# A two-model transformer kernel on one core: first shift by TensorE products, first loads in another order, split latent norm, last expert's outputs one after the other

## The chip, the cores and the metric

The kernel runs on one core of a Trainium2 chip. The metric is the device time of one execution in microseconds (us). Three executions were timed; the median counts. A separate execution was taken by the hardware profiler.

## The reference

Two small transformers of two layers each, one after the other, on 256 tokens of width 1024, all in float32. What matters here:

```python
# first model, layer 0 (ada: shift, scale, gate from the condition c)
mod  = silu(c) @ ada_w[0] + ada_b[0]            # 6 x 1024 values: sh1, sc1, g1, ...
h    = rms_norm(x, attn_norm) * (1 + sc1) + sh1
x    = x + g1 * sparse_mixer(h, ...)            # h @ sp_w_in, attention, @ sp_w_out
...
# second model, layer 0: a pooling branch beside latent attention
proj = u @ in_w                                 # pool | query latents | key-value latents | k_rope
q    = rms_norm(q_lat, q_norm) @ q_up           # 8 heads of 96, rotated
k, v = rms_norm(kv_lat, kv_norm) @ kv_up
y    = concat([pool(...), attend(q, k, v)]) @ out_w
h    = layer_norm(alpha * h + g1 * y)
...
# second model, layer 1: 8 experts, top 2
out  = sum_e combine[:, e] * (silu(t @ wg[e]) * (t @ wu[e])) @ wd[e]
h    = layer_norm(alpha * h + g2 * out)
```

## The kernel before

The activations lie feature-major: `X` is 128 partitions x 8 tiles x 256 tokens. Each engine has its own hand-written program in one block, and semaphores alone order them. SyncE (SP) issues nearly all weight loads, in the order in which they stand in its program; its DMA queue fills a ring `wring` of six chunks of 2 MB. GpSimd (POOL) issues the loads of the ada rows through a ring of two half chunks. Most large products are done in three parts with rounded operands: ScalarE (ACT) makes a rounded copy of half a weight chunk (`round_part`), VectorE (DVE) subtracts it to get the remainder (`part_rest`), and TensorE (PE) multiplies rounded by rounded, rounded weights by the remainder of the activations, and the other way round (`by_token_split`).

**The start.** `ada_rows` holds the ada weights transposed: row t*128+p of a layer has the 1024 weights of output t*128+p. The first 16 blocks of 128 rows are the shift (blocks 0 to 7) and the scale (8 to 15) of the first norm. SP issues: the condition row, spread over 128 partitions (L954), `vec` and `con` (L955, L956), pieces 0, 1 and 2 of the ada rows (`load_first`, L951, two blocks or 1 MB each), `X` (L960), pieces 3 to 7, the first chunk of `sp_w_in` (2 MB, L966), token positions and rotary gains (L967, L968), four more chunks of `sp_w_in`, and so on. ACT applies Silu to the row, squares `X` for the norm (L2042), takes the root, rounds the first half chunk and then, tile by tile, adds the shift (`shifted`, L2060, shown as L2031). DVE makes each block of 128 ada outputs by one multiply and sum over the row (`add_rows`, L2617), 16 of them, with the reciprocal of the norm between; then the gain (`scale_of`), eight tiles of `X` scaled (L2961, shown as L2597), ten small operations on the rotary angles behind a wait for the two small loads (L2962 to L2969), `part_rest` of the first half, eight remainders of the shifted tiles, and so on. PE sums the squares (`sum_squares(0)`), waits until seven ada pieces are done (`ada_used` 7, L1412), runs ten idle products on zeros (L1413) and then the projection.

**The second model's latents.** PE makes pool, query and key-value latents; ACT copies them and their squares; PE sums the squares over partitions in two jobs (`ml_stat[0]` for the queries, 256 columns, `ml_stat[1]` for the keys and values, 512); ACT takes both roots (L2340). DVE first scales `X` by ALPHA (L3143), waits for both roots, takes one reciprocal of 768 columns (L3145), then two query and two key-value tiles (L3148, L3150), and tells PE with `lat_ready`. Then it scales the pool outputs into `OT` (L3156) and does four rotations (`turn`). PE does the pool products, waits for `lat_ready` 1 (L1604) and makes queries, keys and values.

**The last expert.** `products("d", LAST)` is the down product: two output jobs (columns 0 to 511 and 512 to 1023), two halves of the contraction, each rounded parts first. Within a half the loop over the jobs is the innermost one, so both jobs end with the last two matmuls. Then come eight idle products, and `scatter`, which waits for both outputs made by `results` on ACT (L2535) and DVE (L3392).

Helpers record the operations, so many have one line: PE matmuls L1117, ACT copies L2024, ACT Identity L2031, DVE tensor-tensor L2590, scalar-tensor-tensor L2597, tensor-scalar L2593.

Of the kernel before, what the change touches and what calls it, by code (L numbers as in the profile page):

```python
# [28 lines left out]
P = 128  # L29
T = 256  # L30
D = 1024
# [27 lines left out]
for _name, _n in [("attn_norm", 16), ("ffn_norm", 16), ("ada_b", 96),  # L59
                  ("ada_b2", 96), ("ln_g", 32), ("ln_b", 32), ("pool_scale", 4), ("q_norm", 2), ("kv_norm", 2),  # L60
                  ("conv_w", 72), ("conv_b", 24), ("skip", 8), ("moba_q_rest", 1), ("moba_k_rest", 1),
                  ("nsa_q_rest", 1), ("nsa_k_rest", 3), ("out_norm", 1), ("lam", 4), ("fb", 3),
                  ("freq", 1), ("pos_k", 16), ("pos_v", 16), ("diff_q_rest", 1), ("diff_k_rest", 1)]:
    VEC[_name] = (_at, _n)
    _at += _n
# [257 lines left out]
def build(nc, a, out):  # L323

    with ExitStack() as ctx:
# [9 lines left out]
        def sem(name):  # L335
            return ctx.enter_context(nc.semaphore(name))
# [103 lines left out]
        ff_hid_upper, ff_hid_lower, ff_row_loaded = sem("ff_hid_upper"), sem("ff_hid_lower"), sem("ff_row_loaded")  # L440
        lat_ready = sem("lat_ready")
        tsin_arg, tsin_done = sem("tsin_arg"), sem("tsin_done")
        part_upper_made, part_lower_made, part_used = sem("part_upper_made"), sem("part_lower_made"), sem("part_used")
# [22 lines left out]
        def plan_norm(*banks):  # L466
            norm_job.append([J(b) for b in banks])
# [39 lines left out]

        hy_sin, SIN_GROUPS = [], (7, 8, 9)
        plan_norm(6)
        sp_hi = Chunk(ring, dmas=0)  # L510
        sp_w = [Chunk(ring) for _ in range(5)]
        sp_hi_end = Chunk(ring, dmas=0)
        cmp_w = [Chunk(ring), Chunk(ring)]
# [426 lines left out]
        def _(sp):  # L940
# [15 lines left out]
            sp.dma_start(con[:], a["con"]).then_inc(vec_loaded, 16)  # L956
            load_first(0)
            load_first(1)
            load_first(2)
            sp.dma_start(X[:], a["x"]).then_inc(x_loaded, 16)  # L960
            for n in range(3, 8):
                load_first(n)


            w = a["sp_w_in"][0]
            load(sp_w[0], w[:, 2048:2560])  # L966
            sp.dma_start(work[:, 1408:1410].bitcast(I32), a["token_positions"]).then_inc(small_loaded, 16)  # L967
# [147 lines left out]
        def _(pe):  # L1115
# [295 lines left out]
            sum_squares(0)  # L1411
            pe.wait_ge(ada_used, 7)  # L1412
            idle_products(3, 10)  # L1413
            by_token_split(sp_w[0], 0, sp_tok[0], CH, OTupper, Hlower, HI_TILES[0])
# [195 lines left out]
            for j in range(5):  # L1610
                if j < 4:
                    ml_q[j].open(pe)
                    for m in range(2):
                        h = 2 * j + m
                        for k in range(2):
                            last = mm(PS[ml_q[j].b][0:96, m * T:(m + 1) * T], qu[:, k, h * 96:(h + 1) * 96],
                                      QL[:, k, :], k == 0, k == 1)
                    fill(ml_q[j], last)
                if j >= 1:
                    ml_qr[j - 1].open(pe)  # L1620
                    ml_q[j - 1].emptied(pe)
                    fill(ml_qr[j - 1], mm(PS[ml_qr[j - 1].b][0:96, :], mc[0:96, 2048:2144],
                                          Fl[0:96, (j - 1) * 512:j * 512]))
            ml_krr.open(pe)
            ml_kr.emptied(pe)
# [296 lines left out]
            def products(kind, q):  # L1922
# [17 lines left out]
                for h in range(2):  # L1940
                    n = 2 * c.order + h
                    wu, wl = (w.rearrange("p (k n) -> p k n", k=width) for w in (half_upper(n), half_weights(c, h)))
                    pe.wait_ge(upper_made, n + 1)
                    for x in (xu, xl):
                        for k in range(width):
                            for o, job in enumerate(jobs):
                                last = mm(PS[job.b][:, :], x[:, h * width + k, :], wu[:, k, o * CH:(o + 1) * CH],
                                          first and h == 0 and k == 0 and x is xu, False)
                    last.then_inc(upper_used, 1)
                    pe.wait_ge(lower_made, n + 1)  # L1950
                    for k in range(width):
# [70 lines left out]
        def _(act):  # L2022
# [40 lines left out]
            def round_part(c, n, width=CH):  # L2063

                if n % 2 == 0:
                    c.loaded(act)
# [123 lines left out]
            act.wait_ge(vec_loaded, 2 * 16)  # L2190
            act.activation(egate[:, 0:1], C("ones")[:, 0:1], ACT.Silu)
            act.wait_ge(row_loaded, 16)
# [4 lines left out]
            deviation(0)  # L2197
            round_part(sp_w[0], 0)
            shifted(0, mod[:, 0, 0:8], OTupper)
            for n in range(2):  # L2200
# [379 lines left out]
        def _(ve):  # L2580
# [369 lines left out]
            ve.wait_ge(cs_ready, 1)  # L2950
            add_first(0)
            add_first(1)
            for n in range(2, 5):
                add_first(n)
            inverse(0)
            for n in range(5, 8):
                add_first(n)
            ve.wait_ge(ada_used, 8)
            scale_of(0, 8, vec[:, VEC["attn_norm"][0]:VEC["attn_norm"][0] + 8])
            for k in range(KT):  # L2960
                stt(H[:, k, :], X[:, k, :], gsc[:, k:k + 1], rstd[:], ALU.mult, ALU.mult).then_inc(scaled, 1)  # L2961
            ve.wait_ge(small_loaded, SMALL)  # L2962
            ang = work[:, 1416:1432].rearrange("p (q j) -> p q j", q=2)
# [177 lines left out]

            ve.wait_ge(h_tile, H_TILES["pool"] + KT)
            step(ts(X[:], X[:], ALPHA, ALU.mult))  # L3143
            ml_stat[1].emptied(ve)
            step(ve.reciprocal(work[:, 1536:2304], work[:, 1536:2304]))  # L3145
            ml_lat[2].emptied(ve)
            for m in range(2):
                stt(scr[:, m * T:(m + 1) * T], scr[:, m * T:(m + 1) * T], vc("q_norm", m), work[:, 1536:1792], ALU.mult, ALU.mult)  # L3148
                x = scr[:, 512 + m * 512:1024 + m * 512]
                last = stt(x, x, vc("kv_norm", m), work[:, 1792:2304], ALU.mult, ALU.mult)  # L3150
            last.then_inc(lat_ready, 1)
            for n in range(2):
# [410 lines left out]
```

## Time and profile before

| what | us |
|---|---|
| median of 3 runs | 2325.32 |
| lowest, highest | 2323.86, 2338.76 |
| profiled execution, its own time | 2325.35 |
| its span in the profile | 2323.5 |
| PE busy, DVE busy, ACT busy | 2251.1, 1850.3, 1305.3 |

Times are microseconds from the start of the span. PEld is the load of the stationary operand on PE. A float32 matmul on operands that aren't rounded shows as two loads and two matmuls. A row of the timeline may stand for several instructions of one kind (x8); what stands in brackets is the engine's idle time before it and what ended it. The line of a DMA is that of its issue; its time to landing stands in the DMA view.

### The profile page before, as it was taken

To read this page: it belongs to the slowest core of one execution; us is meant where nothing else is said; L and a number is where in the kernel's file an instruction comes from. 1 tells how busy PE (TensorE), PEld (TensorE's weight loads), DVE (VectorE), ACT (ScalarE), POOL (GpSimd) and SP (SyncE) were. 2 spreads that over 40 slices of the span, in tenths; PEclk is the share of its full clock that TensorE was granted. 3 is DMA by queue.
4 is the path that set the end of the run, shared out by engine and by line. 5 is a ranking of instruction groups with operands and counts; after the bars stand their busy time and mean duration, and the time that the engine had idled before them with its cause. 6 is when DMAs were issued, how large, how long until landed. Compare 5 with 4: busy or idle time off the path is not lost.

```text
span 2323.5 us, 31198 instructions
## 1 busy us (share of the span) xinstructions
PE 2251.1 (97%) x12846; PEld 1917.2 (83%) x12860; DVE 1850.3 (80%) x2254; ACT 1305.3 (56%) x1456; POOL 65.3 (3%) x96
## 2 busy tenths in 40 slices
PE   4999999999999999999999999999999999999997
PEld 3867999877999747999877788888888888888886
DVE  7877888865998156878865798988888888889897
ACT  3464433554433234643541587777777777776775
POOL 0000011000001000000000000000000000000000
PEclk9999999999999999999999999999999999999999
DMA  9845888733687712686545499999999999999991
GB/s 376 272 175 190 304 317 303 253 109 127 240 306 288 274 47 100 228 332 238 182 146 188 154 375 347 364 347 362 348 370 343 366 345 365 356 359 354 355 363 74
DMA packets 258763, 635.68 MB, mean 274 GB/s; under 512 B 9175, under 2 KB 21368, under 8 KB 257912
## 3 DMA queue, kind: packets, MB, share of 16 engines
q1 hardware_dynamic: 234104, 539.25, 63.7%
q0 software_dynamic: 24512, 94.38, 10.8%
q8 instruction: 104, 1.70, 0.3%
q14 instruction: 43, 0.35, 0.0%
HBM read 632.55 MB, written 1.05 MB: 273 GB/s over the span
## 4 chain that ended last, share of the span: by engine, by line
PE 84%; DVE 11%; DMA 3%; issue 1%; ACT 1%; SPq 0%; ACTq 0%; DVEq 0%
PE ps L1117 81%; DVE wring_rounded L2590 3%; DVE aring L2617 2%; DMA aring<-in_ada_rows 2%; PE ps L1966 1%; PE ps L1281 1%; DMA F<-in_ada_rows 1%; DVE work L2590 1%; DVE OT L2614 1%; DVE X L2597 1%; DVE work L2593 0%; DVE rstd L2680 0%; PE ps L1256 0%; DVE nmax L2835 0%; DVE H L2590 0%
## 5 line engine op out<-in xcount | busy, mean ns | idle before, releaser
L2590 DVE TENSOR_TENSOR wring_rounded<-wring,scr_rounded 128x2048 fp32r<-128x2048 f32 (+1 forms) x312 | 564.4, 1837 | 83.7 <-ACT scr_rounded L2024 83.7
L2024 ACT ACTIVATE scr_rounded<-wring 128x2048 fp32r<-128x2048 f32 (+1 forms) x312 | 476.5, 1551 | 194.5 <-PE ps L1117 131.0
L1117 PE MATMUL ps<-wring_rounded,OT_rounded 128*128 128x512 f32 (+1 forms) x1184 | 316.7, 392 | 4.5 <-ACT OT_rounded L2031 2.1
L1117 PEld LDWEIGHTS ps<-wring_rounded,OT_rounded 128*128 128x128 f32 x1184 | 220.8, 189 | 50.9 <-ACT wring_rounded L2024 5.0
L2617 DVE CUSTOM_DVE_ANT_0 aring<-aring,F,vec 128x1024 f32<-128x1024 f32 x152 | 188.0, 1283 | 34.7 <-DMA aring<-in_ada_rows 33.7
L2590 DVE TENSOR_TENSOR wring_rounded<-wring,H_rounded 128x2048 fp32r<-128x2048 f32 x84 | 192.2, 2288 | 26.6 <-ACT H_rounded L2024 26.5
L2590 DVE TENSOR_TENSOR wring_rounded<-wring,aring_rounded 128x2048 fp32r<-128x2048 f32 x84 | 192.4, 2290 | 16.3 <-ACT aring_rounded L2024 16.3
L2024 ACT ACTIVATE H_rounded<-wring 128x2048 fp32r<-128x2048 f32 x84 | 161.3, 1921 | 60.8 <-issue 39.5
L2024 ACT ACTIVATE aring_rounded<-wring 128x2048 fp32r<-128x2048 f32 x84 | 161.2, 1919 | 58.1 <-PE ps L1117 58.1
L1117 PE MATMUL ps<-work_rounded,F_rounded 128*128 128x256 f32 x1056 | 169.8, 283 | 0.0
L1117 PE MATMUL ps<-V_rounded,wring_rounded 128*128 128x256 f32 x1056 | 161.5, 285 | 4.2 <-DVE wring_rounded L2590 4.2
L1117 PE MATMUL ps<-V_rounded,scr_rounded 128*128 128x256 f32 x1056 | 159.1, 284 | 1.5 <-ACT V_rounded L2031 1.5
L1117 PEld LDWEIGHTS ps<-V_rounded,wring_rounded 128*128 128x128 f32 x1056 | 143.1, 192 | 7.1 <-DVE wring_rounded L2590 7.1
L1117 PE MATMUL ps<-scr_rounded,OT_rounded 128*128 128x512 f32 x544 | 145.4, 392 | 3.2 <-ACT OT_rounded L2031 2.0
L1117 PE MATMUL ps<-H_rounded,scr_rounded 128*128 128x256 f32 x1056 | 147.5, 284 | 0.0
L1117 PEld LDWEIGHTS ps<-V_rounded,scr_rounded 128*128 128x128 f32 x1056 | 142.8, 193 | 4.2 <-ACT V_rounded L2031 3.0
L1117 PEld LDWEIGHTS ps<-work_rounded,F_rounded 128*128 128x128 f32 x1056 | 145.7, 192 | 0.0
L1117 PEld LDWEIGHTS ps<-H_rounded,scr_rounded 128*128 128x128 f32 x1056 | 136.3, 193 | 0.0
L1117 PEld LDWEIGHTS ps<-scr_rounded,OT_rounded 128*128 128x128 f32 x544 | 100.7, 188 | 24.1 <-issue 3.7
L1117 PE MATMUL ps<-wring_rounded,work_rounded 128*128 128x512 f32 x448 | 120.1, 390 | 0.0
L1117 PE MATMUL ps<-scr_rounded,F_rounded 128*128 128x512 f32 x448 | 119.8, 389 | 0.0
L1117 PE MATMUL ps<-scr_rounded,work_rounded 128*128 128x512 f32 x448 | 114.0, 396 | 0.0
(303 smaller groups left out, 3733.1 us busy)
## 6 DMA issues: line engine op xcount, KB each, us to landing
wring<-in_moe_gate SPq DMA_DIRECT2D x56, 2048.0 KB, 8.3
wring<-in_moe_up SPq DMA_DIRECT2D x56, 2048.0 KB, 8.8
wring<-in_moe_down SPq DMA_DIRECT2D x56, 2048.0 KB, 8.2
aring<-in_ada_rows POOLq DMA_DIRECT2D x88, 1024.0 KB, 7.6
wring<-in_ffn_w_gate SPq DMA_DIRECT2D x10, 2048.0 KB, 9.2
wring<-in_ffn_w_up SPq DMA_DIRECT2D x10, 2048.0 KB, 13.7
wring<-in_ffn_w_down SPq DMA_DIRECT2D x10, 2048.0 KB, 9.2
wring<-in_diff_w_in SPq DMA_DIRECT2D x6, 2048.0 KB, 15.3
```

The lines of the kernel that those rows point to most:

```text
L1117: return pe.matmul(dst, lhsT, rhs, start=start, stop=stop, **kw)
L1281: last = pe.transpose(PS[t[u].b][:, dst:dst + P], pr[:, src:src + P], C("ident"))
L1966: last = pe.transpose(PS[job.b][:, m * P:(m + 1) * P], act_buffer(q)[:, m * P:(m + 1) * P], C("ident"))
L2024: return act.activation(dst, src, ACT.Copy, **kw)
L2590: return ve.tensor_tensor(dst, x, y, op)
L2597: return ve.scalar_tensor_tensor(out=dst, in0=x, scalar=s, in1=y, op0=op0, op1=op1)
L2614: ve.tensor_tensor_reduce(OTl[:, m * D:(m + 1) * D], w[:, m, :], context, 1.0, vec[:, o + m:o + m + 1], ALU.mult, ALU.add, modc[:, first + ...
L2617: last = ve.tensor_tensor_reduce(w[:, m, :], w[:, m, :], row, 1.0, vec[:, o + m:o + m + 1], ALU.mult, ALU.add, mod[:, layer, first + m:fir ...
```

## The change

Five edits in one:

1. SP loads ada pieces 4 and 5, `X`, pieces 6 and 7, then half of the first weight chunk (1 MB, with a semaphore of its own), then pieces 0 to 3, then the other half.
2. The scale still comes from eight row sums on DVE. Of the shift, blocks 0 to 6 come from PE: 56 float32 matmuls, each a 128x128 block of ada weights times one column of 128 condition values, eight per block. For this the host lays those seven blocks out with the contraction on the partitions, and the condition is in `vec` as eight columns. Block 7 stays a row sum on DVE. DVE adds the bias to all seven columns at once.
3. DVE scales `X` before the shift is there; PE runs three idle products instead of ten; ACT rounds the first half chunk on the first half's load alone, and waits for the shift before `shifted`.
4. In the second model DVE norms the query latents on the first root alone and releases PE, then the key-value latents; the ALPHA scaling of `X` moves behind the pool outputs.
5. In the last expert's last half, PE finishes the first output job (six matmuls) before the second.

```diff
@@ SP
-            load_first(0)
-            load_first(1)
-            load_first(2)
+            w = a["sp_w_in"][0]
+            first = wring[:, sp_w[0].slot, :]
+            load_first(4)
+            load_first(5)
             sp.dma_start(X[:], a["x"]).then_inc(x_loaded, 16)
-            for n in range(3, 8):
+            load_first(6)
+            load_first(7)
+            sp.dma_start(first[:, 0:2048]..., w[0:W_FIRST, 2048:2560]...).then_inc(first_half_loaded, 16)
+            for n in range(4):
                 load_first(n)
-            load(sp_w[0], w[:, 2048:2560])
+            sp.dma_start(first[:, 2048:4096]..., w[W_FIRST:D, 2048:2560]...).then_inc(sp_w[0].sem, 16)
@@ PE
             sum_squares(0)
-            pe.wait_ge(ada_used, 7)
-            idle_products(3, 10)
+            pe.wait_ge(cs_ready, 1)
+            ada_job.open(pe)
+            for t in range(7):
+                if t % 2 == 0:
+                    pe.wait_ge(ada0_loaded[t // 2], 16)
+                for k in range(KT):
+                    last = mm(PS[ada_job.b][:, t:t + 1], ada0_buffer(t // 2)[:, t % 2, k * P:(k + 1) * P],
+                              vc("cond", k), k == 0, k == KT - 1)
+            fill(ada_job, last)
+            idle_products(3, 3)
...
+            pe.wait_ge(lat_ready, 2)
             ml_krr.open(pe)
...
                     pe.wait_ge(upper_made, n + 1)
+                    if kind == "d" and q == LAST and h == 1:
+                        pe.wait_ge(lower_made, n + 1)
+                        for o, job in enumerate(jobs):
+                            for x, w in ((xu, wu), (xl, wu), (xu, wl)):
+                                for k in range(width):
+                                    last = mm(PS[job.b][:, :], x[:, h * width + k, :], w[:, k, o * CH:(o + 1) * CH],
+                                              False, w is wl and k == width - 1)
+                            fill(job, last)
+                        continue
@@ ACT
-                if n % 2 == 0:
+                if n == 0:
+                    act.wait_ge(first_half_loaded, 16)
+                elif n == 1 or n % 2 == 0:
                     c.loaded(act)
...
-            act.activation(egate[:, 0:1], C("ones")[:, 0:1], ACT.Silu)
+            act.activation(vc("cond", 0, P, KT), vc("cond", 0, P, KT), ACT.Silu)
...
             round_part(sp_w[0], 0)
+            act.wait_ge(ada_used, 8)
             shifted(0, mod[:, 0, 0:8], OTupper)
@@ DVE, start
-            add_first(0)
-            add_first(1)
-            for n in range(2, 5):
+            for n in range(4, 8):
                 add_first(n)
             inverse(0)
-            for n in range(5, 8):
-                add_first(n)
-            ve.wait_ge(ada_used, 8)
+            ve.wait_ge(ada_used, 4)
             scale_of(0, 8, ...)
             for k in range(KT):
                 stt(H[:, k, :], X[:, k, :], gsc[:, k:k + 1], rstd[:], ...).then_inc(scaled, 1)
+            ve.wait_ge(ada0_loaded[3], 16)
+            w = ada0_buffer(3)[:, 1, :]
+            ve.tensor_tensor_reduce(w, w, crow, 1.0, vc("ada_b", 7), ALU.mult, ALU.add, mod[:, 0, 7:8])
+            ada_job.filled(ve)
+            tt(mod[:, 0, 0:7], PS[ada_job.b][:, 0:7], vc("ada_b", 0, P, 7), ALU.add).then_inc(ada_used, 4)
+            ve.wait_ge(ada_used, 8)
+            ve.sem_inc(ada_job.bank.free, 1)
             ve.wait_ge(small_loaded, SMALL)
@@ DVE, second model
-            ve.wait_ge(h_tile, H_TILES["pool"] + KT)
-            step(ts(X[:], X[:], ALPHA, ALU.mult))
+            ml_stat[0].emptied(ve)
+            step(ve.reciprocal(work[:, 1536:1792], work[:, 1536:1792]))
+            ml_lat[0].emptied(ve)
+            for m in range(2):
+                last = stt(scr[:, m * T:(m + 1) * T], ..., vc("q_norm", m), work[:, 1536:1792], ...)
+            last.then_inc(lat_ready, 1)
             ml_stat[1].emptied(ve)
-            step(ve.reciprocal(work[:, 1536:2304], work[:, 1536:2304]))
+            step(ve.reciprocal(work[:, 1792:2304], work[:, 1792:2304]))
             ml_lat[2].emptied(ve)
...
+            ve.wait_ge(h_tile, H_TILES["pool"] + KT)
+            step(ts(X[:], X[:], ALPHA, ALU.mult))
             ve.wait_ge(tables_loaded, ML_TABLE)
@@ host
+    for t in range(7):
+        arrays["ada_rows"][0, t * P:(t + 1) * P] = x["ada_w"][0][:, t * P:(t + 1) * P].reshape(KT, P, P).transpose(
+            1, 0, 2).reshape(P, D)
```

## Rows read from the trace of the kernel before

**Rows 1.** The page, part 4: the chain that ended last, by engine.

```profile
PE 84%; DVE 11%; DMA 3%; issue 1%; ACT 1%; SPq 0%; ACTq 0%; DVEq 0%
```

**Rows 2.** The chain in order of time, 0 to 160 us: start, us, what.

```profile
58.31 1.25 DVE wring_rounded L2590
...
59.60 10.39 PE ps L1117 x48
```

**Rows 3.** The timeline, 0 to 34 us: three issues of SP (start, us).

```profile
3.85 0.70 SPq L960 DMA_DIRECT2D X<-in_x  x1
...
5.72 2.80 SPq L951 DMA_DIRECT2D V<-in_ada_rows  x1
...
26.44 0.84 SPq L968 DMA_DIRECT2D work<-in_rotary  x1
```

**Rows 4.** The DMA view: the same three, KB each, us from issue to landing.

```profile
X<-in_x SPq DMA_DIRECT2D x1, 1024.0 KB, 13.6
V<-in_ada_rows SPq DMA_DIRECT2D x1, 1024.0 KB, 19.4
...
work<-in_rotary SPq DMA_DIRECT2D x1, 64.0 KB, 9.6
```

**Rows 5.** The timeline, 15 to 95 us: sums of squares, the shift, the angles.

```profile
18.02 5.71 PE L1117 MATMUL ps<-H,con 128*128 128x256 f32 x16 [18.02 <-ACT H L2042]
...
37.49 3.29 ACT L2031 ACTIVATE OT_rounded<-H,mod 128x256 fp32r<-128x256 f32 x8
37.51 0.16 DVE L2964 CAST work<-work 128x2 f32<-128x2 int32 x1
```

**Rows 6.** The timeline: products with one or eight columns, in experts and router.

```profile
1425.45 0.50 PE L1117 MATMUL ps<-pw,F 128*128 128x1 f32 x4
...
1297.24 0.60 PE L1117 MATMUL ps<-rw,H 128*128 128x8 f32 x4
...
1299.94 0.33 PEld L1117 LDWEIGHTS ps<-rw,H 128*128 128x128 f32 x1
...
1300.15 0.33 PEld L1117 LDWEIGHTS ps<-rw,H 128*128 128x128 f32 x1
```

**Rows 7.** Stretches: start:end, us, busy (count) of PE, PEld, DVE, ACT, POOL; PEclk, DMA, GB/s.

```profile
1295.30:1298.70 3.40, 3.08 (x24) 2.30 (x22) 3.40 (x11) 3.07 (x6) 0.00 (x0) 1.00 0.32 116
1298.70:1302.10 3.40, 3.17 (x17) 3.13 (x17) 0.84 (x3) 3.05 (x5) 0.00 (x0) 0.50 0.00 0
```

**Rows 8.** Stretches at the start, same columns.

```profile
24.00:28.00 4.00, 0.00 (x0) 0.00 (x0) 3.96 (x6) 0.24 (x1) 0.00 (x0) 1.00 1.03 410
...
29.00:30.00 1.00, 0.00 (x0) 0.00 (x0) 1.00 (x3) 0.00 (x0) 0.00 (x0) 0.50 1.02 385
```

**Rows 9.** The timeline, 752 to 862 us: the second model's latents.

```profile
768.19 1.23 DVE L2593 TENSOR_SCALAR X<-X 128x2048 f32<-128x2048 f32 x1 [0.77 <-ACT H L2031]
...
809.82 0.47 ACT L2028 ACTIVATE work<-ps,con 128x256 f32<-128x256 f32 x1
...
811.28 4.95 DVE L3145 RECIPROCAL work<-work 128x768 f32<-128x768 f32 x1 [41.86 <-ACT work L2028]
...
818.53 3.69 PE L1117 MATMUL ps<-aring,wring 128*96 128x256 f32 x16 [2.80 <-DVE aring L2597]
...
823.19 0.69 DVE L2590 TENSOR_TENSOR work<-F,aring 96x512 f32<-96x512 f32 x1 [3.15 <-PE ps L1117]
```

**Rows 10.** The timeline, 2264 to 2324 us: the last expert's outputs.

```profile
2299.62 1.07 PE L1117 MATMUL ps<-wring_rounded,work_rounded 128*128 128x512 f32 x4
2300.50 1.27 ACT L2535 ACTIVATE F_rounded<-ps,egate 128x512 fp32r<-128x512 f32 x2 [6.50 <-PE ps L1117]
...
2300.75 1.67 PE L1117 MATMUL ps<-con,zero 128*128 128x512 bf16 x7
...
2301.89 0.74 DVE L2597 SCALAR_TENSOR_TENSOR aring_rounded<-ps,egate,F_rounded 128x512 fp32r<-128x512 f32 x1
...
2302.73 1.29 PE L1117 MATMUL ps<-tables_rounded,F_rounded 128*128 128x256 f32 x9 [0.30 <-issue]
```

More of the change, by code:

```diff
@@ L62 @@
                   ("nsa_q_rest", 1), ("nsa_k_rest", 3), ("out_norm", 1), ("lam", 4), ("fb", 3),
-                  ("freq", 1), ("pos_k", 16), ("pos_v", 16), ("diff_q_rest", 1), ("diff_k_rest", 1)]:
+                  ("freq", 1), ("cond", 8), ("pos_k", 16), ("pos_v", 16), ("diff_q_rest", 1), ("diff_k_rest", 1)]:
     VEC[_name] = (_at, _n)
@@ L441, in build @@
         lat_ready = sem("lat_ready")
+        first_half_loaded = sem("first_half_loaded")
         tsin_arg, tsin_done = sem("tsin_arg"), sem("tsin_done")
@@ L508, in build @@
         hy_sin, SIN_GROUPS = [], (7, 8, 9)
+        ada_job = J(7)
         plan_norm(6)
@@ L511, in build @@
         sp_w = [Chunk(ring) for _ in range(5)]
+        W_FIRST = 4 * P
         sp_hi_end = Chunk(ring, dmas=0)
@@ L956, in _ @@
             sp.dma_start(con[:], a["con"]).then_inc(vec_loaded, 16)
-            load_first(0)
-            load_first(1)
-            load_first(2)
+            w = a["sp_w_in"][0]
+            first = wring[:, sp_w[0].slot, :]
+            load_first(4)
+            load_first(5)
             sp.dma_start(X[:], a["x"]).then_inc(x_loaded, 16)
-            for n in range(3, 8):
+            load_first(6)
+            load_first(7)
+            sp.dma_start(first[:, 0:2048].rearrange("p (k n) -> p k n", k=4),
+                         w[0:W_FIRST, 2048:2560].rearrange("(k p) n -> p k n", p=P)).then_inc(first_half_loaded, 16)
+            for n in range(4):
                 load_first(n)
-            w = a["sp_w_in"][0]
-            load(sp_w[0], w[:, 2048:2560])
+            sp.dma_start(first[:, 2048:4096].rearrange("p (k n) -> p k n", k=4),
+                         w[W_FIRST:D, 2048:2560].rearrange("(k p) n -> p k n", p=P)).then_inc(sp_w[0].sem, 16)
             sp.dma_start(work[:, 1408:1410].bitcast(I32), a["token_positions"]).then_inc(small_loaded, 16)
@@ L1411, in _ @@
             sum_squares(0)
-            pe.wait_ge(ada_used, 7)
-            idle_products(3, 10)
+            pe.wait_ge(cs_ready, 1)
[4 more added lines that the diff above has]
+                for k in range(KT):
+                    last = mm(PS[ada_job.b][:, t:t + 1], ada0_buffer(t // 2)[:, t % 2, k * P:(k + 1) * P], vc("cond", k),
+                              k == 0, k == KT - 1)
+            fill(ada_job, last)
+            idle_products(3, 3)
             by_token_split(sp_w[0], 0, sp_tok[0], CH, OTupper, Hlower, HI_TILES[0])
@@ L3139, in _ @@
             residual(ffn[1]["y"], 1, 40)
-            ve.wait_ge(h_tile, H_TILES["pool"] + KT)
-            step(ts(X[:], X[:], ALPHA, ALU.mult))
+            ml_stat[0].emptied(ve)
+            step(ve.reciprocal(work[:, 1536:1792], work[:, 1536:1792]))
+            ml_lat[0].emptied(ve)
+            for m in range(2):
+                last = stt(scr[:, m * T:(m + 1) * T], scr[:, m * T:(m + 1) * T], vc("q_norm", m), work[:, 1536:1792], ALU.mult, ALU.mult)
+            last.then_inc(lat_ready, 1)
             ml_stat[1].emptied(ve)
-            step(ve.reciprocal(work[:, 1536:2304], work[:, 1536:2304]))
+            step(ve.reciprocal(work[:, 1792:2304], work[:, 1792:2304]))
             ml_lat[2].emptied(ve)
             for m in range(2):
-                stt(scr[:, m * T:(m + 1) * T], scr[:, m * T:(m + 1) * T], vc("q_norm", m), work[:, 1536:1792], ALU.mult, ALU.mult)
                 x = scr[:, 512 + m * 512:1024 + m * 512]
@@ L3543 @@
         columns(x["diff_out_norm"]), upper(x["diff_lambda"]), upper(x["hy_fb1_2"]), upper(x["hy_fb2_2"]),
-        upper(x["hy_fb3_2"]), upper(x["hy_freq_2"]), columns(x["nsa_cmp_pos"]),
+        upper(x["hy_fb3_2"]), upper(x["hy_freq_2"]), columns(x["c"]), columns(x["nsa_cmp_pos"]),
         after_rotary(x["diff_q_norm"]), after_rotary(x["diff_k_norm"])], 1)
```

## The prediction, made before the changed kernel was run

> **What bounds the kernel now.** I read the page's chain by engine first: PE holds 84% of it, DVE 11% [rows 1]. So an edit counts only where it moves one of PE's starts in a stretch where PE waits. Three such stretches are touched; I read the chain in order of time for the first, and the timeline around each. At the start the chain runs over DVE: its last piece there is the remainder at 58.31, and only from 59.60 is it PE, nearly without a break [rows 2]. A shift of DVE's work from 37.5 on therefore moves the whole rest. In the second model's latents PE stands 2.80 us before 818.53, released by DVE [rows 9]. At the end PE waits for the last output, with 0.30 us of idle time before 2302.73 [rows 10].
>
> **The change, part by part.** All sums are made against the profiled execution's own 2325.35 us (the span is 2323.5, so 1.9 lies around it); the median is 2325.32, the same for this purpose.
>
> *Order of the loads.* SP's queue delivers in order. `X` was the fourth large load of 1 MB: issued at 3.85, landing 13.6 later, at 17.45. The piece that goes to `V` was the seventh: 5.72 and 19.4 give 25.1 [rows 3, 4]. Three loads in 7.67 us is 2.56 us for each MB. In the new order `X` is the third (14.9), the last scale piece the fifth (20.0), the half of the weights the sixth (22.5), and the four shift pieces are seventh to tenth: 25.1, 27.7, 30.2, 32.8. The rotary gains land as before, at 26.44 + 9.6 = 36.0, as the bytes ahead of them are the same. So what TensorE is to work on isn't there before 25.1.
>
> *The seven blocks on PE.* 7 blocks x 8 products, each two load-and-matmul pairs (float32; the experts' two products of one column show as four matmuls) are 112 pairs. The nearest rows give two prices. At full clock four matmuls of one column take 0.50 us in all, the last one lasting some 0.17: 0.11 from start to start [rows 6]. At half clock two loads of the router's eight-column products begin at 1299.94 and 1300.15: 0.21 to 0.215 [rows 6]. That is 12.7 us or 24.1 us for the 112, and neither keeps up with the pieces (32 pairs for each MB, 3.6 or 6.9 us against 2.56), so PE and not the DMA sets the end: 25.1 + 12.7 = 37.8, or 25.1 + 24.1 = 49.2.
>
> Which clock? The stretch of the router's products decides. From 1295.30 to 1298.70 PE was busy 3.08 of 3.40 us, but with eight-column products and only some bf16 products of 512 columns between them, the clock full (1.00, 2.4 GHz). In the next stretch it is 0.50 (1.2 GHz), with PE busy 3.17 of 3.40, and it stays there [rows 7]. Busy with thin products did not hold the clock. Here they are thinner (one column), with nothing wide between them. And they begin after a pause: the sum of squares takes 5.7 us [rows 5] and moves ahead with `X` by 2.56, to about 15.4 to 21.1; then PE has nothing until 25.1. Before, after its last matmul at 23.73, the clock was still full up to 28 and half at 29 [rows 8], 4.3 to 5.3 us later. The same delay gives 25.4 to 26.4. So I take half clock from about 26: some eight of the 112 pairs at the cheap price, 23.5 us in all, an end at 48.6. The bounds are 12.7 and 24.1 us.
>
> The Trainium skill, "TensorE: Matmul & The Clock Gate", section "LDWEIGHTS (loading the stationary operand)", has a load of 128 columns take 128/1.2 = 107 ns and names no clock with it. At full clock the row agrees (0.11); at half clock it doesn't (0.215). By the page's figure the 112 pairs would take an estimated 12.0 us at any clock, which is the first rival below.
>
> *From the products to ACT and DVE.* The end of the last matmul, the small sum with the bias on DVE and two semaphores I put at 0.35 us, as for the other small DVE operations (0.16 for the cast [rows 5]). `shifted` then begins at 48.95 instead of 37.49, and DVE's angles, which stand behind the same wait in its program, at about the same time instead of 37.51 [rows 5]: **11.4 us later**. Queued behind DVE's wait are the angles, the remainder of the first half chunk, eight remainders of `H` and all up to 58.31; none of it can go ahead. ACT queues the shift, the sines and the second half chunk behind its own. With the whole block moved alike, the order that made DVE the chain up to 59.60 stays, so 11.4 goes through. The three idle products end at half clock some 1.3 us after 48.6, at 49.9, beside the first shifted tile (49.4); PE isn't on the chain there, so I cost that at nothing (0.5 us if that cover went).
>
> What is taken off DVE (seven row sums), the scaling done ahead, the reciprocal, and the rounding of the first half at 22.5 all end by 28, long before the shift. They would be worth the step from 37.51 to 36.0, where the rotary gains land, if the shift were there. It isn't, so they bring nothing.
>
> *The latents.* The first root ends at 810.29 [rows 9]. A reciprocal of 256 of the 768 columns is a third of 4.95: 1.65; two of the four scalings (2.2 us between 816.23 and 818.53) about 0.8. So `lat_ready` 1 comes at 812.8, while PE is on the pool products until 815.7 (818.53 - 2.80). That wait goes: 2.8 to 3.1, I take **2.9 us**. Late next: the key-value part (3.3 + 1.4) ends at 817.6, the pool outputs (1.65) at 819.2, ALPHA (1.23 [rows 9], hidden before at 768, now in line) at 820.5. DVE then needs the first rotated product, which comes at 823.19 - 2.9 = 820.3, so DVE starts it 0.2 late, and DVE isn't the chain there: PE runs on keys and values to 851. Bounds: 0 (another wait takes over) and 3.1.
>
> *The last expert.* The first output was full at 2300.46, one matmul before the end (2300.69); ACT made its two outputs one after the other from 2300.50, 0.64 each, DVE ended the second at 2302.63, PE began at 2302.73 [rows 10]. Now the first is full five matmuls earlier, and the second output begins at 2300.72 instead of 2301.13. That is 0.4; the idle products stream until about 2302.3 and leave just that. **0.4 us** (bounds 0 and 0.5). Waiting for the remainder weights before the half costs nothing as long as DVE is ahead of PE there, as it was in the row (its four products of the remainder weights began without idle time).
>
> **Sum:** +11.4 - 2.9 - 0.4 = +8.1, so 2325.35 + 8.1 = **2333.4 us**.
>
> **The rivals.**
> *A, the products run at full clock* (the other side: faster). Place: PE between 25.1 and 38. Price: 12.7 us, end at 37.8, shift at 38.1, start +0.6; in all 0.6 - 2.9 - 0.4 = -2.7: 2322.6. It decides as soon as the products end before about 40.9 (37.5 + 3.3), which needs a mean below 0.14 us for each pair. For it: 0.11 is what the only rows with one column show, and the skill's figure. Against it: the clock fell over thin products [rows 7], and the pause of 4 us before.
> *B, the products keep pace with the pieces.* Each below 0.08 us. Then the last piece (32.8) and its row sum on DVE (1.3) would end at 34.3, the angles would begin at 36.1 with the rotary gains: -1.4, in all -4.7: 2320.6. No row shows such a spacing.
> *C, part of the delay is made good later.* The first feed-forward network stands on loads of ada rows; if other loads, then long landed, left them more of the bandwidth, some 4 of the 11.4 us would come back: 2329.4. Against it: those loads are issued when DVE has used the ones before, so they move with it.
> *D, the query latents bring nothing*, a semaphore or a bank holding PE at the old distance: 2336.3. Against it: each of PE's other waits there (pool outputs, root, weights) was met before 815 or has slack as above.
> That the blocks aren't made by PE can't be: nothing else writes them.
>
> **How the numbers follow.** Forecast 0.67, A 0.15, B 0.02, C 0.09, D 0.07. The forecast's own range is 2331 to 2336 (12.7 is outside it, 24.1 us for the products plus the latents' lower end inside). The range given, 2322 to 2337, takes in A, C and D and leaves out B and tails. A measurement of this kernel tells about 1% (23 us) from no change; no case reaches it: within 1% 0.98, faster and slower by more 0.01 each. The sign within that 1% is what the forecast is about: slower, 0.83.
>
> **What would show it.** PE's load of the ada blocks from about 25.1, 112 of them, 0.33 us long and 0.215 apart, with PEclk 0.50 from about 26 to after 49; the first `OT_rounded` of ACT at 49.0, DVE's cast there too, DVE idle before it (about 34 to 48.6); the chain on PE through those products; PE on its own chain from about 71. In the latents a reciprocal of 256 columns ahead of one of 512, and no idle time on PE before the query products. At the end two ACT outputs 1.3 us apart at their starts. Wrong would be: ada products 0.11 apart and a cast before 40 (A); the same delay at 60 but less at 330 (C); PE idle before the query products (D).

## The result, and the profile after

| | before | after |
|---|---|---|
| median of 20 executions each | 2325.80 us (2323.86 to 2338.76) | 2337.82 us (2333.80 to 2357.95) |
| profiled execution (span) | 2325.35 us (2323.5) | 2339.36 us (2337.6) |

The ratio after to before is 1.0040, 95% interval 1.0025 to 1.0055, that is +9.3 us (5.8 to 12.8). The medians are 12.0 us apart, the fastest executions 9.9, the two profiled ones 14.0. The forecast was 2333.4, +8.1: slower, as predicted, and more by 1 us (by the ratio) to 4 us (by the medians; the median of after lies 0.8 us above the stated range of 2322 to 2337). That difference is the second subject of this part.

Where the delay stands along the kernel is read from SP, whose loads are issued when a ring buffer comes free and so mark the same point of the program in every trace. The columns are start, us, what: `sp_w_out` of after, the same of before, then the first `diff_w_in` of after and of before.

```profile
95.84 0.37 SPq L950 DMA_DIRECT2D wring<-in_sp_w_out  x1
```
```profile
84.52 0.37 SPq L947 DMA_DIRECT2D wring<-in_sp_w_out  x1
```
```profile
397.31 0.37 SPq L950 DMA_DIRECT2D wring<-in_diff_w_in  x1
```
```profile
381.28 0.37 SPq L947 DMA_DIRECT2D wring<-in_diff_w_in  x1
```

The times in this part are those of the kernel before. The marks give +11.3 from 85 us on and still at 215, +16.6 at 239, +16.0 at 381, +17.6 from 433 to 808, +14.5 from 990 (behind the latents), +14.3 at 2266 and +14.1 at the end. So the forecast's own terms are all there in their places: +11.3 for +11.4, -3.0 for -2.9, and -0.4 for -0.4 (of which 0.2 us is left at the end). What it lacks is +4.7 between 215 and 381 us and +1.6 between 415 and 433.

**The start.** The chain of waits of after, 0 to 90 us, in order of time:

```profile
5.65 19.33 DMA aring<-in_ada_rows
...
25.12 23.13 PE ps L1123 x112
...
48.34 0.18 DVE mod L2617
...
69.63 1.25 DVE wring_rounded L2617
...
70.92 10.38 PE ps L1123 x48
```

The 112 matmuls of the ada blocks are one piece of the chain, 23.13 us long (the forecast had 23.5), and PE's own chain begins at 70.92 instead of 59.60 [rows 2]. The timeline of the same stretch, with what each waited for in brackets:

```profile
14.62 2.56 ACT L2066 ACTIVATE H<-X 128x256 f32<-128x256 f32 x8 [5.00 <-DMA X<-in_x]
...
15.18 5.72 PE L1123 MATMUL ps<-H,con 128*128 128x256 f32 x16 [15.18 <-ACT H L2066]
...
48.34 0.17 DVE L2617 TENSOR_TENSOR mod<-ps,vec 128x7 f32<-128x7 f32 x1 [14.35 <-PE ps L1123]
...
48.54 3.30 ACT L2055 ACTIVATE OT_rounded<-H,mod 128x256 fp32r<-128x256 f32 x8 [24.17 <-DVE mod L2617]
...
48.65 0.17 DVE L2994 CAST work<-work 128x2 f32<-128x2 int32 x1
```

`X` is there at 14.62, DVE then waits 14.35 us for PE, and the shift and the cast come at 48.54 and 48.65 in place of 37.49 and 37.51 [rows 5]. By stretches (start:end, us, busy and count of PE, PEld, DVE, ACT, POOL; PEclk, DMA, GB/s):

```profile
22.00:25.00 3.00, 0.00 (x0) 0.00 (x0) 2.93 (x7) 1.91 (x1) 0.00 (x0) 1.00 1.03 410
25.00:26.20 1.20, 1.08 (x10) 1.11 (x10) 1.20 (x5) 0.00 (x0) 0.00 (x0) 0.97 1.03 413
26.20:48.00 21.80, 21.80 (x104) 21.80 (x104) 2.50 (x6) 0.00 (x0) 0.00 (x0) 0.50 1.05 387
48.00:53.50 5.50, 5.08 (x13) 3.19 (x14) 4.71 (x14) 4.93 (x12) 1.54 (x2) 0.51 1.06 389
53.50:60.00 6.50, 6.44 (x28) 4.98 (x28) 6.47 (x26) 2.43 (x3) 0.00 (x0) 1.00 1.03 383
```

PE is busy without a gap from 26.20 to 48.00 and its clock is at 0.50 (1.2 GHz) all the while: 21.80 us for 104 pairs is 0.21 each. It is at 1.00 again from 53.50 on, behind products of 512 columns that begin at 48.5.

**The latents and the last expert.** The timeline of the second model's latents:

```profile
827.38 0.47 ACT L2052 ACTIVATE work<-ps,con 128x256 f32<-128x256 f32 x1
...
827.89 1.75 DVE L3173 RECIPROCAL work<-work 128x256 f32<-128x256 f32 x1 [42.90 <-ACT work L2052]
...
833.13 3.62 PE L1123 MATMUL ps<-aring,wring 128*96 128x256 f32 x16
...
836.76 1.22 DVE L2620 TENSOR_SCALAR X<-X 128x2048 f32<-128x2048 f32 x1
...
838.01 0.69 DVE L2617 TENSOR_TENSOR work<-F,aring 96x512 f32<-96x512 f32 x1
```

The root ends at 827.85, 17.56 later than before [rows 9]. The query products stood at 818.53, which would make 836.09; they start at 833.13, without a bracket: the wait is gone, and with it 2.96 us. DVE now scales `X` (836.76) just ahead of the first rotation, which begins at 838.01, 0.2 us later than the same shift would have it, as forecast. And of the end:

```profile
2313.66 0.69 ACT L2562 ACTIVATE F_rounded<-ps,egate 128x512 fp32r<-128x512 f32 x1 [5.37 <-PE ps L1123]
...
2315.01 0.69 ACT L2562 ACTIVATE F_rounded<-ps,egate 128x512 fp32r<-128x512 f32 x1 [0.67 <-PE ps L1123]
2315.05 1.67 PE L1123 MATMUL ps<-con,zero 128*128 128x512 bf16 x7
...
2316.59 1.30 PE L1123 MATMUL ps<-tables_rounded,F_rounded 128*128 128x256 f32 x9
```

The idle products are 14.30 later than before, the products behind them 13.86 [rows 10]: 0.44 us, and the two outputs of ACT begin 1.35 apart. Half of it is gone again when PE's next work begins (2307.42 before, 2321.50 after: 14.08).

**The extra 4.7 us.** Six loads of ada rows are issued by POOL near 200 us, each when DVE has used up the one two before it. The timeline of after:

```profile
198.32 0.71 POOL L1101 DMA_DIRECT2D aring<-in_ada_rows  x1 [70.86 <-DVE mod L2644]
...
204.92 1.28 DVE L2644 CUSTOM_DVE_ANT_0 aring<-aring,vec 128x1024 f32<-128x1024 f32 x1 [4.49 <-DMA aring<-in_ada_rows]
...
212.40 0.70 POOL L1101 DMA_DIRECT2D aring<-in_ada_rows  x1 [3.41 <-DVE mod L2644]
...
212.85 0.37 SPq L950 DMA_DIRECT2D wring<-in_ffn_w_up  x1
...
221.16 1.28 DVE L2644 CUSTOM_DVE_ANT_0 aring<-aring,vec 128x1024 f32<-128x1024 f32 x1 [5.32 <-DMA aring<-in_ada_rows]
...
230.88 2.86 PE L1123 MATMUL ps<-H,con 128*128 128x256 f32 x6 [4.25 <-DVE H L2617]
```

And the same loads in `old_start`, which has the start of the kernel before (it is described below):

```profile
187.17 0.71 POOL L1095 DMA_DIRECT2D aring<-in_ada_rows  x1 [70.87 <-DVE mod L2627]
...
192.42 1.28 DVE L2627 CUSTOM_DVE_ANT_0 aring<-aring,vec 128x1024 f32<-128x1024 f32 x1 [3.14 <-DMA aring<-in_ada_rows]
...
199.90 0.70 POOL L1095 DMA_DIRECT2D aring<-in_ada_rows  x1 [3.41 <-DVE mod L2627]
...
205.18 1.28 DVE L2627 CUSTOM_DVE_ANT_0 aring<-aring,vec 128x1024 f32<-128x1024 f32 x1 [2.28 <-DMA aring<-in_ada_rows]
```

From its issue to its use the first load takes 6.60 us in after and 5.25 in `old_start`. That puts the fourth off to 212.40, 0.45 us ahead of SP's 2 MB of weights (with the old start 199.90, 1.8 us ahead of the same load at 201.70), and it takes 8.76 us instead of 5.28. DVE's residual sums come so late that PE waits 4.25 us for them before the second norm, and in the next stretch the clock is halved. It is halved once more at 439 us, which is the +1.6:

```profile
231.00:234.40 3.40, 3.18 (x8) 2.01 (x10) 0.63 (x3) 1.28 (x3) 0.00 (x0) 0.51 0.82 337
439.20:442.60 3.40, 3.40 (x9) 2.61 (x9) 3.40 (x10) 1.26 (x4) 0.00 (x0) 0.51 1.05 387
```

The two don't belong together. A fall of the clock between 419 and 444 us stands in eight of the thirteen traces taken for this document, that of `old_start` too, where the marks step by the same 1.6; it isn't in the other profile of the changed kernel. So nothing ties the +1.6 to the new start. The late first load is another matter: the DMA view shows what is different about it. The columns are queue and kind, packets, MB and share of the 16 engines. The stretch from its issue to its use in after, and a stretch around the same load in `combined` (below), the only kernel without a delayed start that had it late too:

```profile
q0 software_dynamic: 461, 1.82, 75.7%
q8 instruction: 1, 0.02, 0.9%
```
```profile
q0 software_dynamic: 544, 2.10, 48.4%
q8 instruction: 1, 0.02, 0.5%
```

Besides POOL's queue (q0) one packet of an instruction load (q8), 16 KB, took 0.96 us in after and 0.93 in `combined`, where one of the ada rows takes about 0.16. What this explains is taken up behind the experiments.

### The profile page after: what moved, and what is told of

It is laid out like the page before. It is cut to its first block, busy times and chain, and to the rows that moved or that the text cites. A ratio compares the mean times of both kernels' runs of the same rounds, so it can differ in the third digit from the quotient of the medians.

```text
span 2337.6 us, 31401 instructions
## 1 busy us (share of the span) xinstructions
PE 2271.3 (97%) x12950; PEld 1940.0 (83%) x12965; DVE 1842.3 (79%) x2242; ACT 1305.0 (56%) x1456; POOL 65.3 (3%) x96
## 4 chain that ended last, share of the span: by engine, by line
PE 83%; DVE 11%; DMA 3%; issue 1%; ACT 1%; SPq 0%; ACTq 0%; DVEq 0%
PE ps L1123 81%; DMA aring<-in_ada_rows 3%; DVE wring_rounded L2617 3%; DVE aring L2644 2%; PE ps L1990 1%; PE ps L1287 1%; DVE work L2617 1%; DVE X L2624 1%; DVE OT L2641 1%; DVE work L2620 0%; PE ps L1262 0%; DVE work_rounded L2617 0%; DVE nmax L2862 0%; DVE H L2617 0%; DVE X L2617 0%
## 5 line engine op out<-in xcount | busy, mean ns | idle before, releaser
L2048 ACT ACTIVATE H_rounded<-wring 128x2048 fp32r<-128x2048 f32 x84 | 161.3, 1920 | 60.8 <-issue 39.6
## 6 DMA issues: line engine op xcount, KB each, us to landing
wring<-in_ffn_w_up SPq DMA_DIRECT2D x10, 2048.0 KB, 14.2
```

The lines of the kernel that those rows point to most:

```text
L2048: return act.activation(dst, src, ACT.Copy, **kw)
```

## The experiments

All were timed beside runs of the kernel before on the same chip (its medians there: 2327.39, 2329.38 and 2326.94), so ratios are compared, not medians.

### The parts by themselves

Kernel `old_start` has the edits of the latents and of the last expert alone, `start_only` all the others alone; the diffs are the corresponding parts of the change.

> The kernel before with the latents' and the last expert's edits alone, the start as it was. By the forecast's steps -2.9 and -0.4: 3.3 us under the kernel before, some 2322.5 us, with PE's own chain from 59.6 as before. If the 4 us by which the changed kernel came out above the forecast lie in these two edits (they bring nothing), it is at 2325 to 2326.

Measured: 2321.89 us (12 executions), ratio 0.9983 (0.9965 to 1.0000), -4.0 us. PE's chain starts at 59.74; the marks of its profile are within 0.8 of before up to 738 us (but for -1.4 at 341 to 352, behind a halved clock at 329 that before has and `old_start` hasn't) and -2.2 from 990, a step of -3.0 (PE's query products at 816.35).

> The kernel before with the start's edits alone. By the forecast's steps +11.4: 2337.2. If the excess over the forecast belongs to the start, as the distances between SP's issues suggest (+11.3 at 85 us, but +16 at 397 us), +15 to +16: some 2341. With the old start's kernel the two differences should add up to that of the whole change, some 12.

Measured: 2340.89 us (6), ratio 1.0053 (1.0038 to 1.0069), +12.4 us. The two ratios add up to +8.4, the whole change is +9.3. In the profile of `start_only` the marks are +12.2 at 85 us and +14.7 at 381; the first ada load near 200 us takes 6.57 us, and PE waits 2.2 us before the second norm.

So the loss is all in the start, and the other two edits are a gain of about the size forecast (3.3 us; the interval is 0 to 8).

### What halves the clock

`fill_gap` keeps PE busy up to the ada products (the first addition), `interleave` besides puts a wide product behind each but the last (both additions):

```diff
             sum_squares(0)
+            idle_products(3, 19)
             pe.wait_ge(cs_ready, 1)
...
                               k == 0, k == KT - 1)
+                    if t < 6 or k < KT - 1:
+                        mm(PS[3][:, 0:256], zero[:], con[:, 0:P].bitcast(BF16))
```

> The changed kernel with 19 idle products of 512 columns between the sum of squares and the ada products, so that PE isn't idle before 25.1. Theory (thin products do not hold the clock): the granted clock stays 1.00 up to 25.1 and falls some 4 to 5 us after the last wide product, at about 29 to 30; up to there some 40 pairs at 0.11, the other 72 at 0.207, so the products end at 25.1 + 4.4 + 14.9 = 44.4 instead of 48.25, and the kernel is 3.9 us faster than the changed one. Rival (it was the pause of 4 us that let it fall): clock 1.00 throughout, 112 pairs at 0.11, end at 37.5, the shift at 37.8, and 10.8 us faster. Second rival (the fall was on its way whatever PE did): as the changed kernel, end at 48.

Measured: 2334.44 us (12), ratio 1.0015 (0.9997 to 1.0033). The stretches of `fill_gap`:

```profile
25.20:29.20 4.00, 4.00 (x37) 4.00 (x37) 2.24 (x6) 0.00 (x0) 0.00 (x0) 1.00 1.03 410
29.50:45.00 15.50, 15.50 (x74) 15.50 (x74) 1.29 (x2) 0.00 (x0) 0.00 (x0) 0.50 1.06 382
```

37 pairs at 0.108 us, then 74 at 0.209: PE was never idle, and the clock still fell, 4 us after the last wide product. The shift begins at 45.66, 2.9 us earlier than after. The pause was not the cause; it only brought the fall forward. By the ratios it is 8.8 us faster than the changed kernel on the same chip (`same_again`, 1.0053), not the 3.9 forecast. That fits its first ada load near 200 us, which took 5.54 us: PE didn't wait behind it. (Its profiled execution, 2339.10 us, isn't typical: a clock halved from 139 to 156 us adds 7.5 us to its marks.)

> As fill_gap, and an idle product of 256 columns (0.11 us at full clock) behind each of the 56 ada products. If wide work among the thin holds the clock: 1.00 from 20 to 45, 56 times 0.22 + 0.11 or a little more, end at 43.6 to 46. If it doesn't hold it, all of it at half clock after about 30: an end at 55 or later, and the kernel some 7 us slower than the changed one.

Measured: 2324.49 us (12), ratio 0.9976 (0.9957 to 0.9995), -5.6 us, where the changed kernel on the same chip had 1.0053 (`same_again`, below). Its stretches and groups (line, engine, operation, shapes, count | busy, mean ns):

```profile
15.00:25.20 10.20, 9.97 (x35) 6.61 (x36) 7.83 (x13) 4.61 (x10) 0.00 (x0) 1.00 1.03 404
25.20:39.10 13.90, 13.90 (x170) 13.90 (x169) 3.55 (x8) 0.00 (x0) 0.00 (x0) 1.00 1.05 388
39.10:2301.00 2261.90, 2232.06 (x12817) 1902.57 (x12816) 1814.54 (x2183) 1288.27 (x1427) 65.07 (x92) 1.00 0.75 274
```
```profile
L1123 PE MATMUL ps<-con,zero 128*128 128x256 bf16 x55 | 13.7, 269 | 0.0
...
L1123 PEld LDWEIGHTS ps<-vec,F 128*128 128x128 f32 x48 | 6.0, 188 | 0.0
```

With 55 more products in it the stretch of the ada products is 13.9 us long instead of 23.1: 0.25 us for two thin pairs and a wide product together, less than the 0.33 forecast (an end at 43.6 to 46; it is 39.1). A weight load lasts 188 ns here and 333 ns in after. The shift begins at 39.52, 9.0 us earlier, and PE's chain at 61.90.

### Does a delay grow on its way?

`delay` repeats a scaling on DVE 25 times in the kernel before, `delay_less` 18 times; `same_again` is the changed kernel, profiled a second time.

```diff
-            for n in range(5, 8):
+            for n in range(5, 7):
                 add_first(n)
+            for _ in range(25):
+                step(stt(H[:, 0, :], X[:, 0, :], rstd[:, 0:1], rstd[:], ALU.mult, ALU.mult))
+            add_first(7)
```

> The kernel before with 25 scalings on DVE repeated ahead of the last two row sums, some 11 us of pure delay; the order of the loads, the clock's history and PE's work are otherwise as before. If a delay of this size passes through unchanged, the kernel is later by what the angles' cast is later (11 us for 11 us), at all issues of SP alike. If a delayed start collides with the first feed-forward's loads of ada rows, whatever delayed it, the delay grows to some 15 or 16 us between 136 and 400 us. If the growth belongs to the new start's own edits, it stays 11 here.

Measured: 2341.10 us (6), ratio 1.0061 (1.0042 to 1.0079). The cast is 12.9 us later than before (50.36), the marks give +14.8 at 85 us, +14.2 at 381, +15.3 at 738, +14.4 at the end. So the 2 us between the cast and the first mark weren't foreseen: the clock stays at 0.50 up to 60.8 us (53.4 in after) and 40 of PE's matmuls stand on the chain from 54.66. In between the marks go from 12.6 (1321 to 2266 us) to 15.3, and the steps stand where one of the two traces alone has a halved clock (before at 329 and 1299, `delay` at 436 and 2320). It doesn't grow by itself near 200 us: +14.8 at 125, +14.7 at 239.

> The changed kernel once more, unaltered, with a profile of its own. The start gives +11.3 at SP's issue at 85 us again. Two of the profiles with all seven blocks on PE had the first of six loads of ada rows near 200 us land 6.6 us after its issue, where four others had 5.2 to 5.5, and PE idle 2 to 4 us before the second norm's sum of squares. If that is chance from execution to execution, this profile may have 5.3 us, no such idle time, and +11 at 381 us too; if it goes with the seven blocks, 6.6 us and +14 to +16 at 381 us again.

Measured: 2341.35 us (11), ratio 1.0053 (1.0036 to 1.0071). +12.2 at 85 us, +16.0 at 381, first load 6.8 us, PE's wait 3.4 us: the same picture a third time.

> The kernel before with 18 scalings repeated on DVE instead of 25: 7 times 0.50 us less delay, so +11.3 at SP's issue at 85 us (the other one had +14.8 there and +14.4 at the end). Five profiles whose first load of ada rows near 200 us was issued at 187 to 191 us or at 201.8 had it land 5.2 to 5.5 us later; the three that issued it at 198.3 to 199.2 had 6.6 to 6.8, and all three have the new start with seven blocks. If what counts is the moment (anything that delays by 11 to 12 us), it takes 6.6 us here as well, PE waits 2 to 4 us before the second norm's sum of squares, and the delay at 381 us is +14 or more. If it goes with the new start, 5.3 us, no wait, and +11 there.

Measured: 2342.09 us (12), ratio 1.0053 (1.0033 to 1.0073). +9.9 at 124 us. But the clock was halved from 139 to 153 us in its profile, so the first load was issued at 203.1 and not near 199; it took 5.3 us and PE didn't wait. The moment in question wasn't hit, and this run tells nothing of it.

### A version that beats both

`three_blocks` leaves three of the shift's blocks to PE and gives five to DVE. `angles_ahead` besides issues positions and rotary gains ahead of the four pieces, makes DVE's angles ahead of its five row sums and ACT's sines ahead of the shift. `combined` adds the filling of the clock experiment, six more idle products behind the blocks and a fourth block on PE.

```diff
-            for t in range(7):
+            for t in range(3):
...
-            ve.wait_ge(ada0_loaded[3], 16)
-            w = ada0_buffer(3)[:, 1, :]
-            ve.tensor_tensor_reduce(w, w, crow, 1.0, vc("ada_b", 7), ...)
+            for t in range(3, 8):
+                if t % 2 == 0 or t == 3:
+                    ve.wait_ge(ada0_loaded[t // 2], 16)
+                w = ada0_buffer(t // 2)[:, t % 2, :]
+                ve.tensor_tensor_reduce(w, w, crow, 1.0, vc("ada_b", t), ...)
```

> The changed kernel with three of the shift's blocks on PE and five on DVE, which stood idle 5.29 us there. PE's 48 pairs at 0.207 us from 25.12 end at 35.0, DVE's row sums at 35.1 (the last piece lands at 32.7, two sums of 1.2). The shift then starts at about 35.5 instead of 48.54, and the cast waits for the rotary gains at 36.0 instead of 37.51 in the kernel before: -1.5 to -2.0 at the start, -3.3 for the rest, some 2321. If a new start carries an excess of its own beyond the delay, 2325 or more.

Measured: 2320.29 us (12), ratio 0.9972 (0.9957 to 0.9988), -6.5 us. The timeline of `three_blocks`:

```profile
25.15 10.37 PE L1123 MATMUL ps<-vec,aring 128*128 128x1 f32 x48 [3.72 <-DMA aring<-in_ada_rows]
...
33.94 1.28 DVE L2989 CUSTOM_DVE_ANT_0 F<-F,aring,vec 128x1024 f32<-128x1024 f32 x1
...
35.82 3.30 ACT L2055 ACTIVATE OT_rounded<-H,mod 128x256 fp32r<-128x256 f32 x8 [11.43 <-DVE mod L2617]
```

Both engines end together, at 35.5 and 35.2, and the shift is 1.7 us earlier than in the kernel before.

> The kernel with three blocks on PE, and besides: positions and rotary gains loaded ahead of the shift's pieces, DVE's angles (2.0 us in ten small steps) ahead of its five row sums, ACT's two sines with their table load ahead of the shift. DVE has 1.6 us of idle time between its sums there, so the shift stays at about 36, and what stands behind it on DVE begins 1.9 us earlier: PE's own chain from 56.3 instead of 58.2, and 2.0 us faster than three_blocks, some 2318.5. If the moved loads delay the pieces or the sums end later, 0 to 1 us is left.

Measured: 2319.59 us (9), ratio 0.9951 (0.9933 to 0.9970). PE's chain from 56.52, 1.7 us before that of `three_blocks`.

> The kernel angles_ahead unaltered, beside the next one on one chip. Its median was 2319.6; the profile of it had 27 us more at half clock than that of three_blocks, at 126, 503 and 547 us, where no other profile has all of them. If these falls are chance, they aren't there again and the profiled span is near 2317; if the kernel brings them, they are.

Measured: 2318.33 us (12), ratio 0.9957 (0.9939 to 0.9976), -10.0 us. PE's chain from 57.47, 0.7 us before `three_blocks`. Its profile has halved clock at 327, 423, 501 to 515 and 546 to 553 us; of the three falls in question the last two came again, with a step of 9.4 us in the marks between 433 and 553 both times, and that at 126 us didn't. (In the profile of `angles_ahead` the three together last 38 us and all halved stretches 42 us more than in `three_blocks`, not 27.) Ten of its twelve executions have a mean clock of 0.991 or more, the profiled one 0.988, so most ran without these falls: a span of 2328.9 in a kernel whose median is 2318.3 shows how much one execution may be off. Both intervals lie wholly under 1, but both overlap that of `three_blocks`, so the angles' own gain isn't shown by the times.

> angles_ahead with four blocks on PE instead of three, 19 idle products before them and one of 256 columns behind each: the clock at 1.00 from 15 us on, 32 products at 0.25 us from 25.5 to 33.5, DVE's four sums end at 35.2 (the last piece lands at 32.7), the shift begins at 35.4 instead of 36.2. So 0.8 us faster than angles_ahead, and PE's own chain from 55.7. If a TensorE kept at full clock from the start also spares later falls (the interleaved kernel had none between 15 and 2300 us, the others 7 to 40 us at half clock), 3 to 8 us faster; if those are chance, only the 0.8.

Measured: median 2327.99 us (12; two of them at 2511.84 and 10988.41 us, which the ratio leaves out and nothing in the trace of the one profiled explains; 2326.5 without them), ratio 0.9987 (0.9964 to 1.0011): not faster than `angles_ahead`. Clock 1.00 up to 39 us, but the shift begins at 36.65 (forecast 35.4) and PE's chain at 58.11 (forecast 55.7); the marks are -1.5 at 124 us and +4.1 at 381, and the timeline shows the late load again, without a delayed start:

```profile
207.82 1.28 DVE L2647 CUSTOM_DVE_ANT_0 aring<-aring,vec 128x1024 f32<-128x1024 f32 x1 [4.89 <-DMA aring<-in_ada_rows]
...
217.54 2.90 PE L1123 MATMUL ps<-H,con 128*128 128x256 f32 x6 [3.71 <-DVE H L2620]
```

Here the first load was issued at 185.51 and took 6.8 us, and SP's weights followed the fourth by 0.25 us (199.79 and 200.04).

## Why the prediction was right, and where it fell short

*The order of the loads.* `X` was forecast for 14.9 and came at 14.62; the first shift piece for 25.1, and PE's wait on it ends at 25.12. Reading landings of a queue that delivers in order, by bytes, was good to 0.3 us.

*The seven blocks.* 23.13 us between the bounds of 12.7 and 24.1, from 0.21 at half clock. The rule of choice (thin products don't hold the clock, [rows 7]) is shown by `fill_gap` and `interleave`: PE without a pause lost the clock all the same, with wide products among the thin ones it kept it. The rows that it was read from are weaker: in six of the thirteen traces (`start_only`, `delay`, `delay_less`, `interleave`, `three_blocks`, `angles_again`) the router's products ran without a fall of the clock. That the one profile of before had it was luck. The pause, on which the forecast also leaned, costs only the 2.9 us by which the fall comes earlier. By the figure of the Trainium skill ("TensorE: Matmul & The Clock Gate", section "LDWEIGHTS (loading the stationary operand)"), 107 ns for a load, the blocks would take an estimated 12 us at any clock; it holds at full clock (0.108 each) and not at half (0.209).

*The delay downstream.* The cast at 48.65 for a forecast 49.0, PE's chain at +11.32 for +11.4. The cover of what was taken off DVE was worth nothing, as forecast: DVE stood idle 14.35 us.

*Latents, last expert.* 2.96 for 2.9 and 0.44 for 0.4.

*Rivals.* A (full clock) is out, though `interleave` is nearly what it describes, at a price of 13.9 us for 12.7. B is out. D is out: the wait went. C has the wrong sign: nothing came back between 124 and 400 us. A pure delay (`delay`) had neither shrunk nor grown at 239 us.

*What the forecast lacked* is in "with the whole block moved alike ... 11.4 goes through": true up to 215 us, but beyond it the forecast let the rest of the kernel be a copy of before. In the profile of after +5.3 us came at once, between 215 and 239 us, from one load of ada rows that was used 1.0 us later after its issue than in before (6.60 for 5.55), met SP's weights and made PE wait. How much of it the times hold isn't sharp. The ratio gives +9.3, with 8.1 inside its interval; the medians are 12.0 apart, and `same_again` gives +12.3 (8.4 to 16.5), with 8.1 just outside.

The first load took 6.6 to 6.8 us in four of thirteen profiles: all three of the unaltered new start (after, `same_again`, `start_only`) and `combined`. In the nine others it took 5.2 to 5.6. It isn't the delay (`combined` has none, `delay` has more), and not the seven blocks (`fill_gap`, `interleave` have them). In `combined` and in `angles_again` it was issued at nearly the same moment (185.51 and 184.91) and took 6.8 and 5.3, so the moment alone doesn't make it.

The DMA packets of the thirteen traces sort by the instruction load. In the four, one begins 4.35, 4.50, 4.31 and 2.83 us behind the issue, in the middle of the transfer; in the nine others none begins between 0.2 and 5.3 us behind it. In the four the last packets of POOL's first two loads follow one another at 0.155 us, up to 8.6 to 8.8 us behind the issue (7.3 to 8.1 in eight others), as if one of the 16 DMA engines had been held up for the 0.93 to 0.97 us of the instruction load. `fill_gap` has such a tail too (8.6), with an instruction load just ahead of the issue and the first load used after 5.54, so the tail alone doesn't tell.

The instruction loads go with PE's program: in every trace one begins when PE has started between 1961 and 1990 of its weight loads and products. The first of the six ada loads is issued at 1929 to 1945 of them in the four, just ahead of it, and at 1719 to 1804, 1970 or 2080 in the others. The 112 pairs and seven idle products less put 210 more of them ahead of that load than before. So the late load doesn't look like chance: it came in all three profiles of the new start as it stands; what isn't shown is the cause by itself, as no run moved the instruction load alone. Why PE then waits 4.25, 3.45 and 2.2 us in three profiles of the same start isn't shown either, except that the fourth load takes 6.75 to 8.8 us behind such a first one and 5.3 to 6.4 in the others.

## What to carry to other kernels

A matrix times one vector on TensorE costs its weight loads, and these cost twice as much once the clock is halved, which a stretch of such products brings about by itself: count them at half clock, or put a wide product behind each. Share such work between TensorE and an idle engine until both end with the last load; here five of eight blocks on DVE turned +11 us into -1.7. And add up the effect of an edit by marks along the whole kernel: single executions differ by several us at places that the edit doesn't touch, and only more profiles and ratios over many tell that from the edit. What an edit adds to an engine's program also moves the places where its instructions are loaded; if the marks step far from the edit, look for such a load beside the transfer that is late.

## What the runs showed of the hardware

One wide product of 256 columns behind two thin pairs was nearly free: 0.25 us for the three, where two pairs alone take 0.22 at full clock. A weight load lasts 188 ns there and three of them begin in those 0.25 us, so they overlap; that they run under the wide product is the likely reading and wasn't tried by itself.

An instruction load of one packet of 16 KB takes 0.93 to 0.97 us in the middle of a 1 MB transfer whose own packets take about 0.16, and the four transfers that it fell into were used 1.0 to 1.6 us later than the nine others.

The spread between executions goes with the mean granted clock. The twelve of `interleave` fall into two groups, six at 0.998 (2321.6 to 2322.8 us) and five at 0.995 or 0.996 (2326.2 to 2328.6), with one at 0.993 (2333.6). 0.003 of 2322 us, at half clock, is 14 us, and they cost some 4.6: an estimated third of a us for each us at half clock, averaged over this kernel.
